# Attention step: exponentials scaled in place on GpSimd and turned by one-pass transposes, in place of products with a diagonal of reciprocals

## The reference

```
s_meta = jnp.einsum("bnqkgd,bmkd->bnkgqm", qb, km)
s_band = jnp.einsum("bnqkgd,bnskd->bnkgqs", qb, kband)
s_band = jnp.where(mask[None, :, None, None], s_band, NEG_INF)
p = jax.nn.softmax(jnp.concatenate([s_meta, s_band, s_sink], -1), axis=-1)
ob = (jnp.einsum("bnkgqm,bmkd->bnqkgd", p[..., :N_META], vm)
      + jnp.einsum("bnkgqs,bnskd->bnqkgd", p[..., N_META:N_META + 2 * BLOCK], vband))
```

## Time and profile before

| | |
|---|---|
| time, median of 3 runs | 2829.34 us (2829.26 to 2829.52) |
| time of the profiled execution | 2827.29 us |
| its span in the trace | 2825.6 us |
| TensorE, VectorE, ScalarE, GpSimd busy | 95%, 52%, 33%, 25% of the span |
| attention steps | from about 1794 to 1960 us of the span |

### The profile page before, as it was taken

How to read it: one execution, slowest core, us unless ns; L and a number is a source line. 1 busy time by engine, 2 the same in 40 slices (tenths; PEclk the granted TensorE clock), 3 DMA queues, 4 the chain that set the end, 5 groups by cost and what they waited for, 6 DMA issues and landing times.

```text
span 2825.6 us, 45442 instructions
## 1 busy us (share of the span) xinstructions
PE 2681.5 (95%) x18246; PEld 1815.6 (64%) x18246; DVE 1479.7 (52%) x1798; ACT 945.8 (33%) x1742; POOL 715.3 (25%) x490
## 2 busy tenths in 40 slices
PE   7899999999996999999999879999969999999996
PEld 5566666666663666666666546787646666666664
DVE  6576766686767554554311394674175445443113
ACT  4333333343314223223211254685242332331111
POOL 1043535443255001001112330122540100101214
PEclk9999999999998999999999999998989999999998
DMA  2111111111130111111111011000101111111111
GB/s 105 38 37 38 31 38 31 38 31 38 31 113 15 52 52 45 52 52 45 62 51 51 15 31 52 24 1 3 51 16 52 48 49 52 47 52 62 43 50 60
DMA packets 37987, 123.86 MB, mean 44 GB/s; under 512 B 3312, under 2 KB 12656, under 8 KB 37872
## 3 DMA queue, kind: packets, MB, share of 16 engines
q1 hardware_dynamic: 37872, 122.25, 13.7%
HBM read 118.04 MB, written 4.19 MB: 43 GB/s over the span
## 4 chain that ended last, share of the span: by engine, by line
PE 87%; DVE 8%; ACT 2%; POOL 1%; issue 1%; POOLq 0%; DVEq 0%; DMA 0%; ACTq 0%
PE PS L1603 24%; PE PS L1605 24%; PE PS L1604 24%; PE PS L1775 2%; DVE UB L1154 2%; PE PS L1951 2%; PE PS L1965 1%; PE PS L1967 1%; PE PS L1692 1%; DVE R L1143 1%; POOL hT L584 1%; PE PS L1782 1%; PE PS L1805 1%; PE PS L1767 1%; PE PS L1984 1%
## 5 line engine op out<-in xcount | busy, mean ns | idle before, releaser
L1603 PE MATMUL PS<-R,whi 128*128 128x384 f16 (+1 forms) x3360 | 1047.4, 312 | 23.3 <-DVE wlo L1131 12.3
L1604 PE MATMUL PS<-R,whi 128*128 128x384 f16 (+1 forms) x3360 | 1047.1, 312 | 0.0
L1605 PE MATMUL PS<-R,wlo 128*128 128x384 f16 (+1 forms) x3360 | 1046.9, 312 | 0.0
L1131 DVE SCALAR_TENSOR_TENSOR wlo<-stage,whi 128x1024 f16<-128x1024 f32 (+1 forms) x196 | 265.2, 1354 | 887.3 <-ACT whi L646 887.1
L1603 PE MATMUL PS<-BIG,whi 128*128 128x384 f16 (+1 forms) x1632 | 509.2, 312 | 19.2 <-DVE BIG L1529 8.6
L1604 PE MATMUL PS<-BIG,whi 128*128 128x384 f16 (+1 forms) x1632 | 509.1, 312 | 0.0
L1605 PE MATMUL PS<-BIG,wlo 128*128 128x384 f16 (+1 forms) x1632 | 509.1, 312 | 0.0
L1603 PEld LDWEIGHTS PS<-R,whi 128*128 128x128 f16 x3360 | 330.2, 98 | 198.1 <-issue 22.0
L1604 PEld LDWEIGHTS PS<-R,whi 128*128 128x128 f16 x3360 | 330.1, 98 | 172.3 <-issue 9.9
L1605 PEld LDWEIGHTS PS<-R,wlo 128*128 128x128 f16 x3360 | 330.2, 98 | 167.0 <-issue 1.7
L590 POOL TENSOR_TENSOR BIG<-TT,BIG 128x1040 f32 x44 | 95.1, 2161 | 853.4 <-ACT BIG L1015 853.4
(11 more groups left out here) (212 smaller groups left out, 2871.3 us busy)
## 6 DMA issues: line engine op xcount, KB each, us to landing
stage<-wa SPq DMA_DIRECT2D x164, 512.0 KB, 3.6
stage<-wd SPq DMA_DIRECT2D x32, 704.0 KB, 4.0
hT<-h SPq DMA_DIRECT2D x4, 1536.0 KB, 11.4
out<-hT SPq DMA_DIRECT2D x2, 1536.0 KB, 5.8
hT<-h SPq DMA_DIRECT2D x2, 1088.0 KB, 6.2
out<-hT SPq DMA_DIRECT2D x1, 1024.0 KB, 4.7
pr<-prm SPq DMA_DIRECT2D x1, 328.0 KB, 6.4
BIG<-wdt SPq DMA_DIRECT2D x1, 128.0 KB, 10.3
```

The source lines that it names most:

```text
L1131: eng.scalar_tensor_tensor(out=wlo[:, slot, 0:width], in0=stage[:, slot, 0:width], scalar=WS, in1=whi[:, slot, 0:width], op0=ALU.mult, op1 ...
L1603: eng.matmul(acc, whi[:, slot, ws], x(0, k, b), start=first, stop=False)
L1604: eng.matmul(acc, whi[:, slot, ws], x(1, k, b), start=False, stop=False)
L1605: return eng.matmul(acc, wlo[:, slot, ws], x(0, k, b), start=False, stop=last)
```

## The change

The diagonal matrices are gone. GpSimd instead multiplies the exponentials themselves by their reciprocals, in place in EX, and TensorE turns them with `transpose` against the constant identity. GpSimd's wait for the transposes of two steps before is gone with the buffer INV.

```
-        INV = [T1[:, QPK * P * i:QPK * P * (i + 1)] for i in range(2)]
...
             for n in range(NQD):
-                T = queries(QCH[n][0])
+                e = exped(n)[:, :, 1:]
                 eng.wait_ge(denom_ready, n + 1)
-                if n > 1:
-                    eng.wait_ge(probs_turned, n - 1)
-                eng.tensor_tensor(inv_diag(n), ident[0:T, 0:T].unsqueeze(1).broadcast_to([T, QPK, T]),
-                                  soft(n, 4).unsqueeze(2).broadcast_to([T, QPK, T]), ALU.mult).then_inc(inv_ready, 1)
+                eng.tensor_tensor(e, e, soft(n, 4).unsqueeze(2).broadcast_to(e.shape), ALU.mult).then_inc(probs_normed, 1)
...
             def transposes(n):
 
                 b, g = QCH[n]
-                T, e, inv = queries(b), exped(n), inv_diag(n)
-                eng.wait_ge(inv_ready, n + 1)
+                T, e = queries(b), exped(n)
+                eng.wait_ge(probs_normed, n + 1)
                 if n > 0:
                     eng.wait_ge(probs_copied, n)
                 for r in range(QPK):
                     c = ((r % 2) * 2 + r // 2) * T
                     if b > 0:
-                        eng.matmul(PS[:, 4, c:c + T], e[:, r, 1:1 + P], inv[:, r, :], start=True, stop=True)
+                        eng.transpose(PS[:, 4, c:c + T], e[:, r, 1:1 + P], ident[0:T, 0:T])
                     k0 = 1 if b == 0 else 1 + P
-                    o = eng.matmul(PS[0:own_keys(b), 5, c:c + T], e[:, r, k0:k0 + own_keys(b)], inv[:, r, :],
-                                   start=True, stop=True)
+                    o = eng.transpose(PS[0:own_keys(b), 5, c:c + T], e[:, r, k0:k0 + own_keys(b)], ident[0:T, 0:T])
                 o.then_inc(probs_turned, 1)
```

More of the change, by code:

```diff
@@ L290, in program @@
         scores_ready, scores_masked, max_ready = sem("scores_ready"), sem("scores_masked"), sem("max_ready")
-        exp_ready, denom_ready, inv_ready = sem("exp_ready"), sem("denom_ready"), sem("inv_ready")
+        exp_ready, denom_ready, probs_normed = sem("exp_ready"), sem("denom_ready"), sem("probs_normed")
         probs_turned, probs_copied, values_ready = sem("probs_turned"), sem("probs_copied"), sem("values_ready")
@@ L364, in exped @@
             return EX[n % 2][0:queries(b), :, 0:1 + keys(b)]
-        def inv_diag(n):
-            T = queries(QCH[n][0])
-            return INV[n % 2][0:T, 0:QPK * T].rearrange("p (r t) -> p r t", r=QPK)
         def score_acc(n, w0, w1):
```

## The result

| | before | after |
|---|---|---|
| median of 4 runs each | 2829.3 us (2827.32 to 2829.52) | 2794.55 us (2793.74 to 2798.53) |
| profiled execution, its span | 2827.29, 2825.6 us | 2794.65, 2792.9 us |

By the interval the changed kernel's time reaches up to 2800.7 us, so the whole time alone is not clear of the range; the stages, which repeat far more closely, show where the sum was short. The sign and the limit in the steady steps came as forecast; several sizes did not, that of the tail above all.

A forecast was written before the change was run, and what follows sets the result against it. TensorE's own work was taken to bound the kernel; 20.7 us (steady steps), 2.2 (five beside them), 3.2 (tail) and 0.6 (head) make 26.7 off 2827.29, and 2.05 added for the median gives 2802.5 us, range 2796 to 2816.

The forecast's parts named there:

- What bounds the kernel: Attention's steady steps: TensorE's own work sets the 4.06 us step, of which the turning products take 1.78 us.
- I take 0.11: Steady steps, TensorE: each float32 transpose costs 0.11 us, eight 0.88 us, making TensorE's step 3.16 us.
- ScalarE ends last: Steady steps after the change: ScalarE's queue, 3.24 us a step, sets the step, with the other engines 0.1 us behind.
- GpSimd's operation 1.92 us: Steady steps: GpSimd's multiplication of 1024 elements a partition takes 1.92 us, with 3.2 us kept as upper bound.
- The loop: Steady steps: the chain through the two buffers of exponentials takes 6.27 us for two steps, 3.14 us for one.
- The rival in which GpSimd becomes the limit: Steady steps: a GpSimd operation of 2.9 to 3.2 us sets the step; whole time 2809 to 2818 us, chance 0.19.
- I take 3.30: Steady steps: the new step is 3.30 us, 0.06 over ScalarE's sum; 27 steps gain 20.7 us.
- The distance before and the four after: Five steps around the 27 steady ones: each gains about 0.45 us, 2.2 us together.
- The tail, 3.2 us: Attention's last steps: half the turning instructions save 4.0 us, GpSimd's longer operation takes back 0.87 us; 3.2 us taken.
- The head, 0.6 us: Attention's start: the first transposes save 1.0 us, the next some 0.6, GpSimd's unhidden operation adds 1.0; gain 0.6 us.
- The added 2.05 us: Whole kernel: the median of the runs lies 2.05 us above the profiled execution, turning 2800.6 into 2802.6 us.
- The clock rival: Steady steps: gaps on TensorE make its clock fall; 2850 to 2890 us throughout, 2825 to 2850 if flickering; chance 0.10.

The follow-up runs named there:

- the loaded kernels: The changed kernel with an extra GpSimd multiplication of 256 or 512 elements and a drain ahead of each scaling: 2807.27 us and 2813.42 us.
- the loaded and relieved ScalarE: The changed kernel with one more tiny ScalarE activation in each step, 2800.98 us; and without the sums ScalarE accumulates beside its exponentials, 2789.64 us.
- split scaling: The changed kernel with each scaling in two GpSimd operations of two heads, the first transposes starting after the first operation: 2792.87 us.

## Why the prediction was right in sign and short in size

Of the 7.95 us between 2802.5 and 2794.55, the attention's terms hold 5.5 (32.2 measured, 26.7 summed; 3.5 of it in the tail, 1.1 in the 27 steady steps, 1.1 in the five beside them, less 0.1 in the head), the way from the profiled execution to the median 2.0, and the rest, under 0.5, lies outside the attention, where two executions differ by more.

- **What bounds the kernel.** Right: TensorE's turning products. With products again, and the new scaling around them, the whole gain is gone.
- **"I take 0.11"** for a transpose. Measured 0.096 (a first at 0.10, seven more to 0.77): the row had 128 columns, the kernel has 112. TensorE's step is 3.05, not 3.16. Worth nothing, since ScalarE ends last.
- **GpSimd's operation 1.92 us.** Measured 1.89, never longer. The 3.2 us that bounded it from above was a mean over additions of 2.38 to 3.70 us (L565 before). The loop, 3.14 forecast, is about 3.08 by the loaded kernels. The rival in which GpSimd becomes the limit fell by 0.14 us a step; some 0.3 us more in its operation would have let it in. The 2.2 us worked out from the Trainium skill, "GPSIMD Engine Reference", section 3.1, was an estimate; the trace has 1.89, and the trace decides.
- **"ScalarE ends last", 3.24 us.** Right: 3.22 where the output is one piece, and the loaded and relieved ScalarE show it. **"I take 3.30"**: measured 3.258. The allowance of 0.06 for engines so close together had no row behind it; over the sum of 3.24 the mean step has 0.02, and 27 steps make 1.1 us.
- **The distance before and the four after, 2.2 us.** Measured 3.3. I let ScalarE's full 3.24 us stand for each of the five. They are 3.04, 3.22, 3.23, 3.02 and 2.64: in the last two ScalarE already does the last block's exponentials, which are shorter.
- **The tail, 3.2 us: the step that failed.** Measured 6.7. I put it thus: "Half the instructions take half", 4.0 us less turning on TensorE, less 0.87 for GpSimd. The price was wrong. From the first transpose of a step to its values, the four turnings took 2.03, 2.41, 3.20 and 3.20 us before, 10.8 together; after, they take 0.47, 0.47, 0.47 and 0.78, 2.2 together. That is a quarter or less, not a half, at full clock and at half, and 8.6 us saved where I had put 4.0, with nothing for the first of the four. With so little left TensorE also stopped being the limit, which I had not seen: it waits 1.0 to 1.1 us for the scaling in two steps, ScalarE sets a step of about 2.4 us, and 2.0 of the 8.6 us don't arrive. From first transpose to first transpose the tail's steps were 2.94, 4.03 and 4.81 us, then 7.48 to the output projection; they are 2.55, 2.59, 2.23 and 5.22. The gains 0.4, 1.4, 2.6 and 2.3 us sum to 6.7. Products in the last block alone bring all of it back, and more. "From about 1944 the clock is at 1.2 GHz" was right of the kernel before (it fell at 1944.7); that it fell later in the changed kernel was worth nothing, as the equally short tails with a fall 3.2 and 3.5 us in show.
- **The head, 0.6 us.** Measured 0.5; that GpSimd takes 1.0 back there is what the kernel with products shows (19.07 for 18.07).
- **The added 2.05 us** between profiled execution and median. Not a property of the kernel: in after they are 2794.65 and 2794.55, and the medians of before on three more occasions were 2826.5 to 2829.3. One execution against a median of three was chance.
- **The clock rival**, 0.10. It did not come: the granted clock is 1.00 from 1804 to 1918, and with 57% of TensorE's time in transposes it is whole too. It was nearer than that sounds: with GpSimd loaded the clock did fall, for 3.4 and 6.8 us, where the steady steps begin. The Trainium skill, "TensorE: Matmul & The Clock Gate", Part 4, says of a transpose that "it doesn't count as PE-busy the same way"; by that rule the kernel with four times the transposes was the likeliest to lose its clock. Its trace has 1.00 throughout the steady steps, with 43% of products between the transposes. In the last block the clock falls with either: 4.2, 3.2 and 2.5 us into the tail with products (before, products everywhere, products in the tail), 5.9, 3.5 and 3.2 us in with transposes (after, split scaling, transposes in the tail). Whether transposes alone would hold it no run here shows.

What stays open is why float32 products of 32 columns, with TensorE busy for every microsecond, lose the clock at all, where the float16 ones of the earlier trace rows kept it.

## What to carry to other kernels

Price the stages at the edges with rows of their own shape: here a fifth of the gain came from four steps of 40, because the replaced operation cost four to five times its successor at 32 columns and 2.3 times at 112. The number of columns belongs to what the price is read from. Once the limit is taken away, the sum of what the next engine's queue does gave the new step to 1% here, and a wait that shows up in front of TensorE need not be its limit; loading each engine by a tenth of a microsecond tells which one is. An operation in a loop of two buffers charged half of what was added to it, and only beyond its slack. And where two things changed together, here the length of the turning and the moment at which the clock falls, a run in which only one of them changed tells which one counts.

## What the runs showed of the hardware that was not expected

- A float32 transpose against a float32 product with one moving size: 0.096 for 0.22 us at 112 columns; for a pair at 32 columns, 0.09 for 0.51 at full clock and 0.16 for 0.80 at half.
- The clock fell to 0.50 with TensorE busy for 2.00 of 2.00 us in narrow float32 products, and was 1.00 with it busy for 0.91 of 2.00 in the same stage of the changed kernel. When it fell in the tail, 3.2 or 5.9 us in, made no difference to a tail of 12.6 us.
- With GpSimd given 0.76 or 1.19 us more a step, the clock stood at 0.50 for 3.4 or 6.8 us at the start of the steady steps; in the changed kernel it did not fall there.
- A small ScalarE instruction listed with 0.19 us cost 0.10 between starts, and so did the sum behind each exponential; only the distance between starts adds up.
- A float32 multiplication on GpSimd with a factor repeated along the inner dimension took 1.04 us for 512 elements a partition and 1.89 for 1024, and never more in the attention; the decay in the mixer of the kernel before (L496) took 1.77 us for 512 beside one VectorE operation (L1199), and 1.04 beside another (L1131).
